# Down projection by seven products: evictions ahead of a step's operands, P2's weights resident, ring tiles asked for by ScalarE

## The chip, the core and the metric

The kernel runs on one core of one Trainium2 chip. The metric is the time of one execution in microseconds (us), the median of several runs. All times inside the kernel come from one profiled execution and count from the start of its span.

## The reference, cut to what matters

One inference step of a decoder layer for 1024 prompt positions and 8 samples (1032 columns in all). Its last part is a ConvFFN, and its last product is the one that the change concerns:

```python
def conv_ffn(x, g, w_up, conv_w, conv_b, w_down, buf):
    up = rmsnorm(x, g) @ w_up
    ext = jnp.concatenate([buf.astype(up.dtype), up], axis=1)
    conv = conv_b + sum(ext[:, i:i + t] * conv_w[i] for i in range(CONV_W))
    a, gate = jnp.split(conv, 2, axis=-1)
    y = (jax.nn.silu(gate) * a) @ w_down      # (1032 x 2816) @ (2816 x 1024)
    return y, ext[:, t:]
# and then  x = x + y
```

Everything is float32. The kernel works with the transpose: y has 1024 rows (output features) and 1032 columns (positions), the contraction runs over 2816 = 22 x 128 features.

## The kernel before, in words

**The stage.** The down projection is the last stage, from about 1097 us on. It is computed by Strassen's scheme: features, outputs and columns are each cut in two, and instead of eight half-size products there are seven, in the order P1, P2, P6, P7, P4, P5, P3 (`PHASE`, L483). Each product is a phase of 11 steps (`HK`), so there are 77 steps (`NSTEP`), numbered 0 to 76: P1 is 0 to 10, P2 11 to 21, P6 22 to 32, P7 33 to 43, P4 44 to 54, P5 55 to 65, P3 66 to 76. Here "P6 step 1" is the first step of P6, number 22.

**One step.** The operands are one weight tile (128 x 512) and one activation tile (128 x 516). For float32 accuracy each is split in a high and a low part. ScalarE makes the high parts `bh` (`b_hi`, L2034) and `wh` (`w_hi`, L2045) by copying with rounding; VectorE makes the low parts `bl` (`b_lo`, L2896) and `wl` (`w_lo`, L2901) by subtracting. There are four buffers of each (step number modulo 4), so `b_hi` of step n waits until TensorE is through with step n-4 (`p_done`). TensorE then does 24 matmuls of 128x128 by 258 columns (L1558 to L1560): four output blocks j, two column chunks, three products high-high, high-low, low-high. All eight banks of PSUM hold the four blocks j.

**Sums.** Most phases need sums or differences of tiles. VectorE makes them in place (`down_sum`, L2912): T1 to T4 of activation tiles, S1, S2, S2b, S3, S4 of weight tiles. Three lists say in which of its rounds VectorE makes each: `SUM_BEFORE` (ahead of `b_lo`), `SUM_BETWEEN` (between `b_lo` and `w_lo`), `SUM_BEHIND`. In round n VectorE makes bl and wl of step n. Of weight: S3 = w_a - w_b (in w_a), S2 = raw tile - w_a, S1 = w_b + raw tile, S4 = raw tile - w_a. S2 for step n+1 stands ahead of `b_lo(n)` in round n, S4 too.

**Weight tiles.** `w_a` (11 tiles) and `w_b` (11 tiles) are resident; `wr` is a ring of four raw tiles. In P2, P6, P4 and P3 the raw tile comes through the ring: SyncE asks for it (`ring_load`, L955) once step n-4 is done. So P2 uses the tile as it is, P4 too, P6 and P3 after S2 or S4.

**Between phases.** PSUM is emptied when a phase ends: after P1 by ScalarE (`p1_copy`, L2050, four copies to `u_p1`, written behind `w_hi` of step 13), after the others by VectorE (`evict`, L2984, four additions, block j each, written at the end of the round of the third step of the next phase, behind its `b_lo` and `w_lo`). TensorE waits for each bank before the first matmul of the next phase that writes it (`bank_free`, L1536). `pair_done` tells that a block j of a phase's last step is through.

**Order on the queues.** Each engine runs its instructions in the order written. SyncE (SP) issues, from 1108 us: the second halves of activation tiles (`act_load2`, L935, at most four in flight), tile 21, then `x_quarter` (L960, 1 MB each, the residual into xq0, xq1, xq2, each waiting until the one before has landed), and between them the ring tiles and `wb_load` (L948, w_b, one per P2 step). Later `y_store` (L965) writes finished quarters.

Of the kernel before, what the change touches and what calls it, by code (L numbers as in the profile page):

```python
# [98 lines left out]
def build(nc, t):  # L99
# [5 lines left out]
    with ctx:  # L105
# [391 lines left out]
        def weight(st):  # L497
            ph, k = PHASE[st // HK], st % HK
            return (w_a[k] if ph in ("P1", "P7") else w_b[k] if ph == "P5" else wr[st % 4])[:, :]

        RING_NO = {}
        for ph_ in ("P1", "P2", "P6", "P4", "P3"):
            for k_ in range(HK):
                RING_NO[step_of(ph_, k_)] = len(RING_NO)
# [3 lines left out]
        for k_ in range(HK):  # L508
            SUM_BEFORE[5 + k_ if k_ < 6 else 2 * k_ - 1].append(("T3", k_))
            SUM_BEHIND[5 + k_ if k_ < 6 else 2 * k_ - 1].append(("T2", k_))  # L510
            SUM_BEHIND[13 + k_].append(("S3", k_))
# [8 lines left out]
        VEC_NO = {}  # L520
        for st_ in range(NSTEP):
            for x_ in SUM_BEFORE[st_] + SUM_BETWEEN[st_] + SUM_BEHIND[st_]:
# [89 lines left out]
        def act_total(f):  # L612
            return 16 * (12 + f // 4 + 1)
        SET_END = {}
# [13 lines left out]
        def _(sp):  # L628
# [308 lines left out]
            def down_w(mi, f):  # L937
                return dnL[f, :, 512 * mi:512 * mi + 512]

# [5 lines left out]
            def wb_load(k):  # L945
                if k >= 4:
                    sp.wait_ge(S(f"tok_ld{k % 4}"), wb_total(k - 4))
                sp.dma_start(w_b[k][:, :], down_w(1, k)).then_inc(S(f"tok_ld{k % 4}"), 16)  # L948

            def ring_load(st):  # L950
                ph, k = PHASE[st // HK], st % HK
                mi = 1 if ph in ("P6", "P4") else 0
                n = RING_NO[st]
                sp.wait_ge(S("p_done"), NPROD + st - 3)
                sp.dma_start(wr[st % 4][:, :], down_w(mi, HK + k)).then_inc(S(f"ring_ld{n % 4}"), 16)  # L955
# [44 lines left out]
            for f in H2_ORDER[7:-1]:  # L1000
                act_load2(f)
# [4 lines left out]
            for st in range(HK, NSTEP):  # L1006
                ph, k = PHASE[st // HK], st % HK
                if st in RING_NO:
                    ring_load(st)
                if ph == "P2":  # L1010
                    if k == 1:
                        x_quarter(1, xq1, 0, 1)
                    if k == 3:
                        x_quarter(2, xq2, 1, 1)
                    wb_load(k)
# [551 lines left out]
        def _(act):  # L1567
# [454 lines left out]

            def b_hi(st):
# [12 lines left out]
            def w_hi(st):  # L2036
                ph, k = PHASE[st // HK], st % HK
                if ph in ("P1", "P2", "P4"):
# [1173 lines left out]
```

## Time and profile before

| | before |
|---|---|
| median of 3 runs | 1364.05 us (1361.47 to 1366.6) |
| the profiled execution's own time | 1361.91 us |
| its span | 1360.2 us |
| TensorE busy / VectorE / ScalarE | 95% / 78% / 44% of the span |
| DMA, mean over the span | 156 GB/s |

### The profile page before, as it was taken

How to read it: one execution, taken by the hardware profiler on the slowest of the kernel's cores; microseconds unless marked ns; L12 is line 12 of the kernel's file. 1: busy time of each engine (PE TensorE's matmuls, PEld its weight loads, DVE VectorE, ACT ScalarE, POOL GpSimd, SP SyncE). 2: the span in 40 equal slices, each digit the busy share in tenths (PEclk: the TensorE clock that was granted, in tenths of full speed). 3: DMA queues.
4: the chain of work that ended last, by engine and by line, in shares of the span. 5: the costliest groups of instructions: out<-in, count | busy, mean ns of one | idle time of the engine just before them, and what ended most of it. 6: DMA issues, size and time to landing. Idle time of an engine off the chain costs nothing.

```text
span 1360.2 us, 25417 instructions
## 1 busy us (share of the span) xinstructions
PE 1286.8 (95%) x9535; PEld 1181.0 (87%) x9535; DVE 1062.1 (78%) x1615; ACT 601.7 (44%) x1025; POOL 207.2 (15%) x207
## 2 busy tenths in 40 slices
PE   7999999989989999999999999999999996899988
PEld 5888787777667678899999999999999996899988
DVE  7678879988988767567687787788788885687955
ACT  7623111355657565344544434434434442333432
POOL 1420034322323430100101101101101000000000
PEclk9999999969999899999899999999999997999999
DMA  9878766689999773431221221221221497421212
GB/s 317 293 219 241 198 179 181 205 234 263 288 316 341 226 219 88 153 102 51 79 94 56 87 93 56 86 94 57 85 94 55 161 311 249 141 78 32 86 63 86
DMA packets 144279, 212.69 MB, mean 156 GB/s; under 512 B 13870, under 2 KB 93128, under 8 KB 143876
## 3 DMA queue, kind: packets, MB, share of 16 engines
q1 hardware_dynamic: 128564, 160.44, 37.8%
q0 software_dynamic: 10688, 38.80, 9.3%
q10 hardware_dynamic: 4904, 11.81, 3.1%
q8 instruction: 76, 1.25, 0.4%
q14 instruction: 47, 0.39, 0.1%
HBM read 180.68 MB, written 29.82 MB: 155 GB/s over the span
## 4 chain that ended last, share of the span: by engine, by line
PE 67%; DVE 13%; DMA 8%; issue 4%; SPq 3%; POOL 3%; ACT 1%; ACTq 1%; POOLq 0%; DVEq 0%
PE ps L1482 8%; PE ps L1483 8%; PE ps L1484 8%; PE ps L1558 5%; PE ps L1560 4%; PE ps L1559 4%; PE ps L1324 4%; PE ps L1265 3%; PE ps L1267 3%; PE ps L1266 3%; DMA upr<-in_w_upL 2%; PE ps L1347 2%; DMA wr<-in_w_down 1%; PE ps L1305 1%; DMA act<-scr_act 1%
## 5 line engine op out<-in xcount | busy, mean ns | idle before, releaser
L1558 PE MATMUL ps<-bh,wh 128*128 128x258 f32 x616 | 179.0, 291 | 30.1 <-DVE xq L2984 16.1
L1482 PE MATMUL ps<-hhi,uph 128*128 128x258 f32 x704 | 201.1, 286 | 1.6 <-DVE ug L2856 0.9
L1483 PE MATMUL ps<-hlo,uph 128*128 128x258 f32 x704 | 200.0, 284 | 0.0
L1484 PE MATMUL ps<-hhi,upl 128*128 128x258 f32 x704 | 199.7, 284 | 0.0
L1559 PE MATMUL ps<-bl,wh 128*128 128x258 f32 x616 | 176.5, 287 | 0.0
L1560 PE MATMUL ps<-bh,wl 128*128 128x258 f32 x616 | 175.9, 285 | 0.0
L1558 PEld LDWEIGHTS ps<-bh,wh 128*128 128x128 f32 x616 | 119.3, 194 | 31.4 <-issue 29.5
L1482 PEld LDWEIGHTS ps<-hhi,uph 128*128 128x128 f32 x704 | 134.3, 191 | 3.0 <-DVE ug L2856 2.0
L1483 PEld LDWEIGHTS ps<-hlo,uph 128*128 128x128 f32 x704 | 134.5, 191 | 0.0
L1484 PEld LDWEIGHTS ps<-hhi,upl 128*128 128x128 f32 x704 | 134.2, 191 | 0.0
L1265 PE MATMUL ps<-whi,hhi 128*128 128x512 f32 (+1 forms) x336 | 126.3, 376 | 0.9 <-PE ps L1267 0.6
L1267 PE MATMUL ps<-whi,hlo 128*128 128x512 f32 (+1 forms) x336 | 124.9, 372 | 0.0
L1266 PE MATMUL ps<-wlo,hhi 128*128 128x512 f32 (+1 forms) x336 | 124.6, 371 | 0.0
L1560 PEld LDWEIGHTS ps<-bh,wl 128*128 128x128 f32 x616 | 120.3, 195 | 0.0
L1559 PEld LDWEIGHTS ps<-bl,wh 128*128 128x128 f32 x616 | 120.1, 195 | 0.0
L1324 PEld LDWEIGHTS ps<-vst,pts 128*128 128x128 f32 x576 | 74.1, 202 | 31.5 <-issue 27.2
L3146 POOL TENSOR_TENSOR upr<-upr 128x512 f32<-128x512 f32 x22 | 29.5, 1343 | 450.5 <-DMA upr<-in_w_upL 367.5
L1900 ACT ACTIVATE uph<-upr 128x1024 fp32r<-128x1024 f32 (+1 forms) x66 | 79.3, 1202 | 41.7 <-DMA upr<-in_w_upL 37.4
L2776 DVE TENSOR_TENSOR upl<-upr,uph 128x1024 fp32r<-128x1024 f32 (+1 forms) x66 | 92.2, 1396 | 0.3 <-ACT uph L1900 0.2
L1324 PE MATMUL ps<-vst,pts 128*128 128x65 f32 x576 | 81.3, 289 | 9.2 <-DVE oN L2481 8.1
L2168 DVE TENSOR_TENSOR ring<-ring,qb 128x1024 f32<-128x1024 f32 x64 | 78.0, 1219 | 9.4 <-DMA ring<-in_cache_a_k 7.8
L3083 POOL DMA_INDIRECT vring<-in_cache_a_v,gtab x64 | 61.7, 964 | 140.4 <-PE ps L1347 136.4
(359 smaller groups left out, 3393.0 us busy)
## 6 DMA issues: line engine op xcount, KB each, us to landing
upr<-in_w_upL SPq DMA_DIRECT2D x88, 256.0 KB, 3.4
ring<-in_cache_a_k SPq DMA_DIRECT2D x170, 128.0 KB, 3.2
scr_act<-va SPq DMA_DIRECT2D x22, 516.0 KB, 2.6
wr<-in_w_down SPq DMA_DIRECT2D x44, 256.0 KB, 2.7
ring<-in_cache_a_k ACTq DMA_DIRECT2D x86, 128.0 KB, 3.0
act<-scr_act SPq DMA_DIRECT2D x36, 258.0 KB, 4.0
wst<-in_w_in SPq DMA_DIRECT2D x32, 256.0 KB, 3.9
x<-in_xT SPq DMA_DIRECT2D x16, 258.0 KB, 5.5
```

The source lines that it names most:

```text
L1265: pe.matmul(out, lh, whi[:, sl, 0:w], start=(kc == 0), stop=False)
L1266: pe.matmul(out, lh, wlo[:, sl, 0:w], start=False, stop=False)
L1267: i = pe.matmul(out, ll, whi[:, sl, 0:w], start=False, stop=(kc == KC - 1))
L1324: i = pe.matmul(ps[:, 6, 0:HD + 1], pts[:, g % 2, j, :], vst[:, hp % 2, j, VCOL[H % 2]], start=(j == 0), stop=(j == nb - 1))
L1482: pe.matmul(out, hi_, r_hi[:, cs], start=(first and i == 0), stop=False, skip_group_check=not first)
L1483: pe.matmul(out, hi_, r_lo[:, cs], start=False, stop=False, skip_group_check=not first)
L1484: m = pe.matmul(out, lo_, r_hi[:, cs], start=False, stop=(i == 3), skip_group_check=not first)
L1558: pe.matmul(out, hi_, bh[n][:, cs], start=(fresh and k == 0), stop=False, skip_group_check=not fresh)
L1559: pe.matmul(out, hi_, bl[n][:, cs], start=False, stop=False, skip_group_check=not fresh)
L1560: m = pe.matmul(out, lo_, bh[n][:, cs], start=False, stop=(k == HK - 1), skip_group_check=not fresh)
L1900: act.activation(uph[p % 2][:, a:b, :], upr[p % 2][:, a:b, :], ACT.Copy).then_inc(S("st_hi"), 1)
L2776: dve.tensor_tensor(upl[p % 2][:, a:b, :], upr[p % 2][:, a:b, :], uph[p % 2][:, a:b, :].bitcast(f32), ALU.subtract).then_inc(S("st_lo"), 1)
```

## The change

1. **Evictions.** The four evictions of a phase (all but P1's and P3's) move one round earlier and to the front: in the round of the second step of the next phase (two steps after the phase's last; `EVICT_AT`) VectorE evicts blocks 0 and 1, makes bl, evicts blocks 2 and 3, makes the sums in between, wl, and only then the sums that stood ahead of bl. ScalarE's four copies after P1 move likewise: two ahead of `b_hi(12)`, two between it and `w_hi(12)`.
2. **P2's weights resident.** The 11 raw tiles of P2 go into `w_b` ahead of the stage's second phase, each between two of the `act_load2` of SyncE; the ring no longer serves P2. The tiles that `w_b` held before (bottom weights for S3) are loaded over them, each once `w_lo` of the P2 step is made. S3 moves one round later (rounds 14 to 24, was 13 to 23), T3 and T2 one round later or two.
3. **Ring tiles asked for by ScalarE.** `ring_load` moves from SyncE's list to ScalarE's, directly ahead of `b_hi` of the same step, with the same condition (step n-4 done). The remaining 33 ring tiles (P6, P4, P3) go this way.

```diff
--- before.py
+++ after.py
@@ -496,19 +496,19 @@
 
         def weight(st):
             ph, k = PHASE[st // HK], st % HK
-            return (w_a[k] if ph in ("P1", "P7") else w_b[k] if ph == "P5" else wr[st % 4])[:, :]
+            return (w_a[k] if ph in ("P1", "P7") else w_b[k] if ph in ("P2", "P5") else wr[st % 4])[:, :]
 
         RING_NO = {}
-        for ph_ in ("P1", "P2", "P6", "P4", "P3"):
+        for ph_ in ("P1", "P6", "P4", "P3"):
             for k_ in range(HK):
                 RING_NO[step_of(ph_, k_)] = len(RING_NO)
         SUM_BEFORE = {st: [] for st in range(NSTEP)}
         SUM_BETWEEN = {st: [] for st in range(NSTEP)}
         SUM_BEHIND = {st: [] for st in range(NSTEP)}
         for k_ in range(HK):
-            SUM_BEFORE[5 + k_ if k_ < 6 else 2 * k_ - 1].append(("T3", k_))
-            SUM_BEHIND[5 + k_ if k_ < 6 else 2 * k_ - 1].append(("T2", k_))
-            SUM_BEHIND[13 + k_].append(("S3", k_))
+            SUM_BEFORE[6 + k_ if k_ < 5 else 2 * k_ + 1].append(("T3", k_))
+            SUM_BEHIND[6 + k_ if k_ < 5 else 2 * k_ + 1].append(("T2", k_))
+            SUM_BEHIND[14 + k_].append(("S3", k_))
             SUM_BEFORE[step_of("P6", k_) - 1].append(("S2", k_))
             SUM_BEFORE[step_of("P7", k_)].append(("T4", k_))
             SUM_BETWEEN[step_of("P4", k_)] += [("S1", k_), ("S2b", k_)]
@@ -518,8 +518,10 @@
         SUM_BEHIND[34].append(("x22", 0))
         SUM_BEHIND[38].append(("x21", 0))
         VEC_NO = {}
+        EVICT_AT = {step_of(ph_, HK - 1) + 2: ph_ for ph_ in PHASE[1:-1]}
         for st_ in range(NSTEP):
-            for x_ in SUM_BEFORE[st_] + SUM_BETWEEN[st_] + SUM_BEHIND[st_]:
+            first_, second_ = (SUM_BETWEEN, SUM_BEFORE) if st_ in EVICT_AT else (SUM_BEFORE, SUM_BETWEEN)
+            for x_ in first_[st_] + second_[st_] + SUM_BEHIND[st_]:
                 VEC_NO[x_] = 2 * FT + len(VEC_NO) + 1
         MV0, ST0 = 21, 3 * FT
         EVICT = ["P2", "P6", "P7", "P4", "P5", "P3"]
@@ -611,6 +613,8 @@
 
         def act_total(f):
             return 16 * (12 + f // 4 + 1)
+        def down_w(mi, f):
+            return t["w_down"][f, :, 512 * mi:512 * mi + 512]
         SET_END = {}
         for k_ in range(NV):
             if vset(k_)[2]:
@@ -934,25 +938,18 @@
                     sp.wait_ge(S("act_st"), 16 * FT)
                 sp.dma_start(act_t[f][:, col_half(1)], scr_act[f, :, col_half(1)]).then_inc(S(f"x_ld{i % 4}"), 16)
 
-            def down_w(mi, f):
-                return dnL[f, :, 512 * mi:512 * mi + 512]
-
             def wa_load(k):
                 if k >= 4:
                     sp.wait_ge(S(f"ring_ld{k % 4}"), ring_total(k - 4))
                 sp.dma_start(w_a[k][:, :], down_w(0, k)).then_inc(S(f"ring_ld{k % 4}"), 16)
 
-            def wb_load(k):
-                if k >= 4:
-                    sp.wait_ge(S(f"tok_ld{k % 4}"), wb_total(k - 4))
-                sp.dma_start(w_b[k][:, :], down_w(1, k)).then_inc(S(f"tok_ld{k % 4}"), 16)
-
-            def ring_load(st):
-                ph, k = PHASE[st // HK], st % HK
-                mi = 1 if ph in ("P6", "P4") else 0
-                n = RING_NO[st]
-                sp.wait_ge(S("p_done"), NPROD + st - 3)
-                sp.dma_start(wr[st % 4][:, :], down_w(mi, HK + k)).then_inc(S(f"ring_ld{n % 4}"), 16)
+            def wb_load(n):
+                if n >= 4:
+                    sp.wait_ge(S(f"tok_ld{n % 4}"), wb_total(n - 4))
+                if n >= HK:
+                    sp.wait_ge(S("st_lo"), ST0 + step_of("P2", n - HK) + 1)
+                src = down_w(0, HK + n) if n < HK else down_w(1, n - HK)
+                sp.dma_start(w_b[n % HK][:, :], src).then_inc(S(f"tok_ld{n % 4}"), 16)
 
             def x_quarter(i, dst, mi, ni):
                 if i:
@@ -997,22 +994,22 @@
             act_store(FT - 1)
             sp.wait_ge(S("aff"), 2 * FT)
             sp.dma_start(t["o_u10"], u10[:, :, :]).then_inc(S("out"), 16)
-            for f in H2_ORDER[7:-1]:
-                act_load2(f)
+            for k in range(HK):
+                wb_load(k)
+                if k < 10:
+                    act_load2(H2_ORDER[7 + k])
             sp.wait_ge(S("act_st"), 16 * FT)
             act_load(21)
             act_load2(21)
             x_quarter(0, xq0, 0, 0)
             for st in range(HK, NSTEP):
                 ph, k = PHASE[st // HK], st % HK
-                if st in RING_NO:
-                    ring_load(st)
-                if ph == "P2":
-                    if k == 1:
-                        x_quarter(1, xq1, 0, 1)
-                    if k == 3:
-                        x_quarter(2, xq2, 1, 1)
-                    wb_load(k)
+                if ph == "P2" and k == 1:
+                    x_quarter(1, xq1, 0, 1)
+                if ph == "P2" and k == 3:
+                    x_quarter(2, xq2, 1, 1)
+                if HK < st <= 2 * HK:
+                    wb_load(st - 1)
                 if st == step_of("P6", 3):
                     for j in range(4):
                         y_store("P2", j)
@@ -2020,6 +2017,12 @@
                 act.wait_ge(S("tap"), 6 * p + 4)
                 act.activation(vg[:, :], vg[:, :], ACT.Silu).then_inc(S("silu"), 1)
 
+            def ring_load(st):
+                ph, k = PHASE[st // HK], st % HK
+                n = RING_NO[st]
+                act.wait_ge(S("p_done"), NPROD + st - 3)
+                act.dma_start(wr[st % 4][:, :], down_w(1 if ph in ("P6", "P4") else 0, HK + k)).then_inc(S(f"ring_ld{n % 4}"), 16)
+
             def b_hi(st):
                 ph, k = PHASE[st // HK], st % HK
                 if st < 3:
@@ -2035,9 +2038,11 @@
 
             def w_hi(st):
                 ph, k = PHASE[st // HK], st % HK
-                if ph in ("P1", "P2", "P4"):
+                if ph in ("P1", "P4"):
                     n = RING_NO[st]
                     act.wait_ge(S(f"ring_ld{n % 4}"), ring_total(n))
+                elif ph == "P2":
+                    act.wait_ge(S(f"tok_ld{k % 4}"), wb_total(k))
                 elif ph in ("P6", "P3"):
                     act.wait_ge(S("s_vec"), VEC_NO["S2" if ph == "P6" else "S4", k])
                 elif ph == "P5":
@@ -2083,11 +2088,16 @@
             affine_a(FT - 1)
             silu(FT - 1)
             for st in range(4, NSTEP):
+                if st == HK + 1:
+                    p1_copy(0)
+                    p1_copy(1)
+                if st >= HK and st in RING_NO:
+                    ring_load(st)
                 b_hi(st)
+                if st == HK + 1:
+                    p1_copy(2)
+                    p1_copy(3)
                 w_hi(st)
-                if st == HK + 2:
-                    for j in range(4):
-                        p1_copy(j)
 
 
         @block.vector
@@ -2937,7 +2947,7 @@
                     dve.wait_ge(S("mv_lo"), MV0 + step_of("P6", k) + 1)
                     summed(top1, bot2, top1, ALU.subtract)
                 if name == "S3":
-                    dve.wait_ge(S(f"tok_ld{k % 4}"), wb_total(k))
+                    dve.wait_ge(S(f"tok_ld{(HK + k) % 4}"), wb_total(HK + k))
                     dve.wait_ge(S("st_lo"), ST0 + step_of("P1", k) + 1)
                     summed(wa, wa, wb, ALU.subtract)
                 if name == "S2":
@@ -3040,18 +3050,25 @@
             taps(FT - 1, ua, va, FT - 1, 2)
             gated(FT - 1)
             for st in range(4, NSTEP):
-                for name, k in SUM_BEFORE[st]:
-                    down_sum(name, k)
+                ph = EVICT_AT.get(st)
+                if ph:
+                    evict(ph, 0)
+                    evict(ph, 1)
+                else:
+                    for name, k in SUM_BEFORE[st]:
+                        down_sum(name, k)
                 b_lo(st)
+                if ph:
+                    evict(ph, 2)
+                    evict(ph, 3)
                 for name, k in SUM_BETWEEN[st]:
                     down_sum(name, k)
                 w_lo(st)
+                if ph:
+                    for name, k in SUM_BEFORE[st]:
+                        down_sum(name, k)
                 for name, k in SUM_BEHIND[st]:
                     down_sum(name, k)
-                ph = PHASE[(st - 3) // HK]
-                if (st - 3) % HK == HK - 1 and ph in EVICT:
-                    for j in range(4):
-                        evict(ph, j)
             for j in range(4):
                 evict("P3", j)
 
```

## Rows read from the trace of the kernel before

**Rows 1.** The page: the span, and TensorE's busy time, share and instructions

```profile
span 1360.2 us, 25417 instructions
PE 1286.8 (95%) x9535; PEld 1181.0 (87%) x9535; DVE 1062.1 (78%) x1615; ACT 601.7 (44%) x1025; POOL 207.2 (15%) x207
```

**Rows 2.** Timeline of TensorE, first matmuls of steps and the stage's last: start, length

```profile
1097.45 0.28 PE L1558 MATMUL ps<-bh,wh 128*128 128x258 f32 x1
...
1113.60 0.36 PE L1558 MATMUL ps<-bh,wh 128*128 128x258 f32 x1 [1.69 <-DVE wl L2901]
...
1143.12 0.55 PE L1558 MATMUL ps<-bh,wh 128*128 128x258 f32 x1 [12.14 <-ACT u_p L2050]
...
1147.94 0.28 PE L1558 MATMUL ps<-bh,wh 128*128 128x258 f32 x1
...
1150.81 0.28 PE L1558 MATMUL ps<-bh,wh 128*128 128x258 f32 x1
...
1182.07 0.55 PE L1558 MATMUL ps<-bh,wh 128*128 128x258 f32 x1 [5.39 <-DVE xq L2984]
...
1218.22 0.36 PE L1558 MATMUL ps<-bh,wh 128*128 128x258 f32 x1 [2.77 <-DVE xq L2984]
...
1254.00 0.36 PE L1558 MATMUL ps<-bh,wh 128*128 128x258 f32 x1 [2.59 <-DVE xq L2984]
...
1322.57 0.55 PE L1558 MATMUL ps<-bh,wh 128*128 128x258 f32 x1 [5.33 <-DVE xq L2984]
...
1356.49 0.28 PE L1560 MATMUL ps<-bh,wl 128*128 128x258 f32 x1
```

**Rows 3.** Stretches: us, busy of PE, PEld, DVE, ACT, POOL, PEclk, DMA share, GB/s

```profile
360.00:385.00 25.00, 21.21 (x190) 16.00 (x189) 21.66 (x45) 12.01 (x23) 8.98 (x9) 1.00 1.07 305
...
1114.00:1120.00 6.00, 6.00 (x53) 6.00 (x52) 6.00 (x11) 1.56 (x3) 0.00 (x0) 1.00 0.99 351
...
1126.00:1134.00 8.00, 4.98 (x42) 4.78 (x41) 1.38 (x3) 0.00 (x0) 0.00 (x0) 0.98 0.97 326
...
1322.57:1327.80 5.23, 5.23 (x24) 5.23 (x25) 1.66 (x3) 0.00 (x0) 0.00 (x0) 0.50 0.54 202
```

**Rows 4.** The chain that ended last, DMA pieces: start us, length us, what

```profile
1126.30 7.41 DMA xq<-scr_x
...
1134.70 7.14 DMA wr<-in_w_down
...
1176.71 2.61 DMA wr<-in_w_down
```

**Rows 5.** Timeline of VectorE, end of P2, and one sum over a quarter

```profile
1179.42 0.69 DVE L2912 TENSOR_TENSOR wr<-wr,wa 128x512 f32<-128x512 f32 x1 [0.24 <-DMA wr<-in_w_down]
...
1181.23 2.50 DVE L2984 TENSOR_TENSOR xq<-ps,xq 128x516 f32<-128x516 f32 x4
...
1213.35 2.31 DVE L2912 TENSOR_TENSOR xq<-xq,u_p 128x2064 f32<-128x2064 f32 x1
```

**Rows 6.** Timeline of VectorE and of ScalarE in P3: S4, then its w_hi

```profile
1330.78 0.69 DVE L2912 TENSOR_TENSOR wr<-wr,wa 128x512 f32<-128x512 f32 x1 [6.56 <-DMA wr<-in_w_down]
...
1331.51 0.63 ACT L2045 ACTIVATE wh<-wr 128x512 fp32r<-128x512 f32 x1 [2.77 <-DVE wr L2912]
```

**Rows 7.** Timeline of ScalarE where it issues DMAs (key pages, an earlier stage)

```profile
106.43 0.46 ACT L1657 ACTIVATE zo<-ps,rsx 128x256 f32<-128x256 f32 x1
106.58 1.35 ACTq L432 DMA_DIRECT2D ring<-in_cache_a_k  x2
...
250.86 0.47 ACT L1666 ACTIVATE sq<-ps,rsx 128x256 f32<-128x256 f32 x1
251.21 3.89 ACTq L432 DMA_DIRECT2D ring<-in_cache_a_k  x4
```

**Rows 8.** Issue to landing: the 44 ring tiles; the w_b tile issued at 1140.98

```profile
DMA to landing us min/median/max: 2.5/2.7/7.6
...
DMA to landing us min/median/max: 5.6/5.6/5.6
```

## The prediction, made before the changed kernel had run

> **What bounds the kernel now.** I read the page first: TensorE is busy for 95% of the span [rows 1], so only its idle time can be won. The timeline of TensorE then gives the places [rows 2]. A step takes 2.86 us when nothing waits: the next first matmul comes 1150.81 - 1147.94 = 2.87 later. The 77 steps go from 1097.45 to 1356.6 [rows 2]: 259.1 us, against 77 x 2.86 = 220.2, so some 39 us are lost. They lie at six places: step 5, 1.9; P1 to P2, 12.3; P2 to P6, 5.5; P6 to P7, 2.9; P7 to P4, 2.8; P5 to P3, 5.5 (the idle times in brackets plus 0.1 to 0.2 for the modelled tail of the last matmul), and 0.6 in two small ones. After four of them the clock has fallen: the first step of P3 takes 5.1 us at a granted 0.50, which is the 1.2 GHz level [rows 3]. That adds 2.0, 1.3, 1.6 and 2.6 us. The sum is 39.
>
> Why they wait: at the end of P2 (1176.7) SP asks for ring tile 25, which lands 2.6 later [rows 4], then come S2, bl, wl and only at 1181.23 the evictions [rows 5]. P2 itself starts late because its ring tiles stand behind 1 MB quarters on SP: 7.4 us for the first, then 7.1 for tile 13 behind the second [rows 4], and `p1_copy` stands behind `w_hi(13)`.
>
> **The change, part by part.** T is always the end of a phase's last step.
>
> *Step 5.* T3(0) leaves round 5, where it held bl(5) up until an activation half had landed. bl(5), wl(5) are then ready by 1110, and the step is due at 1111.7 instead of the 1113.6 of rows 2. Gain 1.9; no later T3 comes too late (round 6: wl at 1113.4, due 1114.6).
>
> *P1 to P2.* P2's weights are resident before step 11 (due 1128.9), and p1_copy stands ahead. Copies 0 and 1 follow blocks 0 and 1 of step 10, the last ends near 1130.0, `w_hi(12)` near 1130.5, wl(12) 1131.3, due 1131.8. So steps 11 to 14 run through, until 1140.3. But on SP the 11 new tiles (2.88 MB) stand ahead of the first quarter, and the DMA engines were moving 351 and 326 GB/s there, all but full [rows 3]: 8.2 to 8.8 us, less up to 1.7 for a slack stretch between. The first quarter landed at 1133.7 [rows 4]; now near 1141.0 (1140 to 1142). The second quarter waits for that, and `wb_load` for S3(0) stands behind it: issued 0.4 later and landing 5.6 later (the row of a w_b tile just behind a quarter [rows 8]), at 1147.0. S3(0) is in round 14, ahead of bl(15). VectorE then does S3, T3, bl, wl, each 0.61 apart: step 15 starts at 1149.7 instead of 1140.3, 9.4 us idle, and about 2.0 for the clock, as after the 12.1 before. The stall thus moves four steps back and shrinks from 14.3 to 11.4: gain 2.9 only. S3(2) waits once more, for a tile behind the third quarter, until about 1152.5; step 17 is due at 1157.4, so this is hidden. P2 ends at T = 1171.7, was 1176.5.
>
> *Evictions.* With blocks 0 and 1 evicted ahead of bl, behind what is in round n-1, the wait moves off TensorE's path. An eviction takes 0.62 (2.50 for four [rows 5]), a quarter of a step 0.72, so once the first is in time the others are. P6 to P7: VectorE is free, the first eviction ends 1.3 ahead of T, gain 4.5. P7 to P4: gain 2.8, less 0.25 for wl of P4 step 1, which now stands behind four evictions, bl, S1 and S2b (T+3.1, due T+2.9). P4 to P5: 0.1. P2 to P6 and P5 to P3: round n-1 holds S2 (S4) for a tile that ScalarE asked for only after `w_hi` of the step before; S2 ends at T-1.1, bl, wl at T+0.1, at P6 an S3 as well, then the eviction: TensorE starts at T+1.55 and T+0.9 instead of T+6.9 and T+8.1 (clock included): gain 5.35 and 7.2. In P7 the sum x22 (2.31 us [rows 5]) follows closely on the evictions and makes wl(35) 0.8 late.
>
> *Ring tiles by ScalarE: the term that decides.* SP asked for tile n as soon as step n-4 was done, whatever else went on. On ScalarE the request stands behind `w_hi(n-1)`. In P6 and P3 `w_hi(n-1)` waits for S2(n-1), that for its tile, and that for its request. So a circle closes, which the kernel before did not have:
> - S2 or S4 start to `w_hi` start: 0.73 (1330.78 to 1331.51 [rows 6]).
> - `w_hi` start to the DMA's issue: not in the trace for this pair. ScalarE issued key pages 0.15 and 0.35 after the start of the activation ahead of them, before it had ended [rows 7]. I take 0.25; no less than 0.15 is likely, and 0.65 if the issue waits for the 0.63 of the activation.
> - issue to the next S2: landing 2.7 in the median, 2.5 at least [rows 8]; tile 25 took 2.71 from TensorE's end (1176.71) to S2 (1179.42) [rows 4, 5]. Most of the spread lies above, so I take 2.87, and 3.0 as the upper end.
>
> Together 3.85 us a step (3.5 to 4.4) against TensorE's 2.86. Because S2(n+1) stands ahead of bl(n) and wl(n), TensorE has no reserve: step n starts 1.3 after S2(n+1) ends. P6: steps 22 and 23 on T+1.55 and T+4.5; S2(25) can only be asked for after S2(24), which now stands behind the evictions, so step 24 starts at T+10.2, 2.9 late; then seven steps at 3.85. A pause of 2.9 may cost the clock, as it did at P7 [rows 2]; the steps behind it have 1.0 of slack each, so I add nothing. P6 ends at T+43.3, plus 0.5 for the residual quarter beside it: 10.8 beyond its stall and its 31.4. P3 the same, from T+0.9: step 68 at T+9.6, end T+42.2, 9.9 beyond. In P4 `w_hi` needs the tile alone: circle 0.3+2.7+0.05 = 3.05, a lag of 0.2 a step, covered by the three steps of lead. The 33 issues themselves lie in ScalarE's idle time (44% busy [rows 1]). SP, rid of ring waits, gives out the residual quarter and the stores earlier; nobody waits for them.
>
> *Sum.* Gains: 1.9 + 2.9 + 5.35 + 4.5 + 2.8 + 0.1 + 7.2, and 0.5 for a small wait in P6: 25.3. Losses: 10.8 + 9.9 + 0.8 + 0.25 = 21.7. Net -3.6 us. Against the profiled execution's 1361.9 this is 1358.3; the three runs have their median at 1364.05, 2.1 higher, so I say 1360.4.
>
> No row speaks against ScalarE's queue as such. The Trainium skill ("DMA: Bandwidth & Descriptors", Issuing engines are not separate DMA queues) says that a request from another engine only saves the issuing sequencer's time. By that alone the move would be free and the sum would be 21 us lower. The page does not treat what stands ahead of the request.
>
> **The rivals.**
>
> *A. The requests don't hold each other up.* If ring tiles always land well ahead, P6 and P3 lose nothing: 1360.4 - 20.7 = 1339.7; with the quarters earlier too, 1328. For it: the same condition in the code. Against it: the order of ScalarE's list, which is not a question of size. 6 in 100.
>
> *B. Slower: the issue waits for the activation.* Then a circle is 0.73 + 0.65 + 3.0 = 4.4 and the 16 steps that hang on it cost 0.55 more each: +8.8. The pauses of 3.5 at step 24 and step 68 then bring the clock down as well, as a pause of 2.8 did at P7 and one of 2.6 did not [rows 2]; half is absorbed, since the steps behind have 1.5 of slack each: +2. That gives 1371. It decides from a circle of 4.3 on. Against it: rows 7. 11 in 100.
>
> *C. Slower still: the clock falls in every circle.* TensorE would pause about 1.0 of each 3.85 us. With 5.1 us for a step at 1.2 GHz [rows 3] the step would be longer than the circle: 16 x 1.3 = 21 more, 1381. Against it: from 360 to 385 TensorE was 85% busy in short pieces and the clock stayed 1.00 [rows 3]; at 74% it is less sure. 4 in 100. The Trainium skill ("TensorE: Matmul & The Clock Gate", HAM oscillation — how this bites in real kernels) describes a loop whose wait for a DMA throttles the engine anew in each round. That was with longer waits than compute; here the wait is the shorter.
>
> *D. A shorter circle, 3.5 to 3.6, or quarters that land at 1139.* A circle of 3.55 takes 16 x 0.3 = 4.8 off, quarters 2 us earlier some 1.5 more: 1354. It is the lower end of my own terms. 19 in 100.
>
> **How the numbers follow.** The forecast with its terms near their values has 60 in 100: 1360.4, from 1354 to 1367. With half of D's and B's reach the range is 1352 to 1369. A measurement of this kernel can tell about 0.5% (6.8 us) from no change. Faster by more than that, below 1357.2 us (0.995 times 1364.05): A, D and a tail of the forecast, 0.28. Slower, above 1370.9: B's upper part, C, 0.12. Within: 0.60.
>
> **What would show it.** P2: idle time of TensorE not at step 11 but at step 15, about 9 us, released by wl behind an S3 that waited for w_b's tile. P6 and P3: first matmuls of steps 25 to 31 and 69 to 75 some 3.85 apart, VectorE's S2 and S4 waiting for the ring tile each time, and ScalarE's request right behind `w_hi`. P7, P4, P5: steps 2.86 apart, no pause at their starts but 0.8 at P7's third step. PEclk 1.00 in P6 and P3. The prediction is wrong if ring requests go out ahead of `w_hi` of the step before, if the circle is under 3.6 or over 4.1, or if the first quarter lands before 1139.

## The result, and the profile after

The changed kernel takes 1352.0 us (median of 7, 1348.2 to 1356.0) against 1364.05 (median of 7, 1361.5 to 1370.4): ratio 0.991, 95% interval 0.988 to 0.993. That is 12 us less, where the forecast was 3.6 less and "within 0.5%" the likeliest; 1352.0 lies on the lower end of the stated range. The mechanism that the forecast rested on is in the trace; its price was too high.

The span is 1349.3 us, against 1360.2 [rows 1]. This is the whole stage as one stretch, first of the kernel before and then of the changed one (columns: stretch, length, busy time of TensorE, weight loads, VectorE, ScalarE, GpSimd, then granted clock, DMA share, GB/s):

```profile
1097.45:1356.61 259.16, 229.04 (x1850) 227.67 (x1848) 182.54 (x281) 90.12 (x157) 0.00 (x0) 0.95 0.38 123
```

```profile
1094.92:1345.50 250.58, 230.82 (x1850) 226.81 (x1848) 181.18 (x281) 90.13 (x157) 0.00 (x0) 0.97 0.38 128
```

The stage is 8.6 us shorter, with the same work in it. It also starts 2.5 us earlier, though everything ahead of it is the same program: that part is no effect of the change (more on it below, with the second traces). The timeline of TensorE, first matmuls of steps 15, 22, 24, 27, 33, 35, 44, 66, 68 and 74; it answers [rows 2]:

```profile
1147.09 0.55 PE L1555 MATMUL ps<-bh,wh 128*128 128x258 f32 x1 [8.64 <-DVE wl L2911]
...
1170.75 0.36 PE L1555 MATMUL ps<-bh,wh 128*128 128x258 f32 x1 [1.13 <-DVE xq L2994]
...
1178.97 0.36 PE L1555 MATMUL ps<-bh,wh 128*128 128x258 f32 x1 [1.94 <-DVE wl L2911]
...
1191.04 0.36 PE L1555 MATMUL ps<-bh,wh 128*128 128x258 f32 x1 [0.93 <-DVE wl L2911]
...
1210.51 0.28 PE L1555 MATMUL ps<-bh,wh 128*128 128x258 f32 x1
...
1217.17 0.36 PE L1555 MATMUL ps<-bh,wh 128*128 128x258 f32 x1 [0.78 <-DVE wl L2911]
...
1242.96 0.28 PE L1555 MATMUL ps<-bh,wh 128*128 128x258 f32 x1
...
1306.70 0.36 PE L1555 MATMUL ps<-bh,wh 128*128 128x258 f32 x1 [0.27 <-DVE xq L2994]
...
1314.94 0.36 PE L1555 MATMUL ps<-bh,wh 128*128 128x258 f32 x1 [1.96 <-DVE wl L2911]
...
1336.18 0.36 PE L1555 MATMUL ps<-bh,wh 128*128 128x258 f32 x1 [0.50 <-DVE wl L2911]
```

Read against [rows 2]: the 12.1 at step 11 has become 8.6 at step 15; the 5.4, 2.8, 2.6 and 5.3 at the starts of P6, P7, P4 and P3 have become 1.1, nothing, nothing and 0.3. New are a pause of 1.9 at the third step of P6 and of P3 and one of 0.2 to 0.9 at most of the steps after it, all released by `wl`. So P6 and P3 stretch to 39.8 and 38.8 us, where 11 x 2.86 is 31.4. The stretches of P6 and P3 show TensorE busy for 89% and 90%, the clock near full:

```profile
1170.75:1210.51 39.76, 35.32 (x264) 33.68 (x265) 26.95 (x42) 13.12 (x23) 0.00 (x0) 0.96 0.31 107
1306.70:1345.50 38.80, 34.78 (x264) 33.46 (x264) 21.76 (x35) 9.88 (x17) 0.00 (x0) 0.96 0.27 88
```

The pause at step 15 has its reason on SyncE and in the chain. The first quarter lands 8.59 after its request; only then does `wb_load` get its turn, and S3(0) on VectorE has waited 11.82 us for that tile (chain of the changed kernel, then timeline of VectorE):

```profile
1129.92 8.59 DMA xq<-scr_x
...
1138.98 5.42 DMA wb<-in_w_down
...
1144.43 0.69 DVE L2922 TENSOR_TENSOR wa<-wa,wb 128x512 f32<-128x512 f32 x1 [11.82 <-DMA wb<-in_w_down]
```

And this is the circle, in P3: S4 on VectorE, `w_hi` and the next request on ScalarE, and the next S4 when the tile has landed (timelines of VectorE and ScalarE, in order of time):

```profile
1330.54 0.69 DVE L2922 TENSOR_TENSOR wr<-wr,wa 128x512 f32<-128x512 f32 x1 [1.70 <-DMA wr<-in_w_down]
...
1331.26 0.63 ACT L2050 ACTIVATE wh<-wr 128x512 fp32r<-128x512 f32 x1 [2.44 <-DVE wr L2922]
1331.27 0.33 ACTq L2024 DMA_DIRECT2D wr<-in_w_down  x1
...
1334.13 0.69 DVE L2922 TENSOR_TENSOR wr<-wr,wa 128x512 f32<-128x512 f32 x1 [1.69 <-DMA wr<-in_w_down]
...
1334.86 0.63 ACT L2050 ACTIVATE wh<-wr 128x512 fp32r<-128x512 f32 x1 [2.44 <-DVE wr L2922]
1334.86 0.34 ACTq L2024 DMA_DIRECT2D wr<-in_w_down  x1
```

It goes round in 3.59 us here, and between 3.3 and 3.6 elsewhere, with two exceptions in P6. One turn of 4.0 holds the sum x12. One of 4.8, from 1176.92 to 1181.68, holds a tile that took 3.93 to land: the last 1 MB quarter had gone out on SyncE 2.46 us ahead of it (timeline of SyncE, then chain):

```profile
1175.20 0.38 SPq L957 DMA_DIRECT2D xq<-scr_x  x1
...
1177.66 3.93 DMA wr<-in_w_down
```

The link that no row of before showed, from `w_hi` to the request, is 0.00 to 0.01 us in every turn.

### The profile page after: what moved, and what is told of

Its sections match the earlier page's. It is cut to its first block, busy times and chain, and to the rows that moved or that the text cites. A ratio compares the mean times of both kernels' runs of the same rounds, so it can differ in the third digit from the quotient of the medians.

```text
span 1349.3 us, 25428 instructions
## 1 busy us (share of the span) xinstructions
PE 1287.0 (95%) x9535; PEld 1178.0 (87%) x9535; DVE 1058.6 (78%) x1615; ACT 601.5 (45%) x1025; POOL 207.9 (15%) x207
## 4 chain that ended last, share of the span: by engine, by line
PE 54%; DVE 17%; DMA 13%; issue 5%; SPq 5%; POOL 4%; ACT 2%; ACTq 1%; DVEq 0%; another core or an unknown queue 0%; POOLq 0%
PE ps L1479 9%; PE ps L1480 8%; PE ps L1481 8%; DMA wr<-in_w_down 4%; PE ps L1321 3%; PE ps L1555 3%; PE ps L1557 2%; PE ps L1556 2%; POOL rsn L3087 2%; DMA upr<-in_w_upL 2%; PE ps L1344 2%; DMA ring<-in_cache_a_k 2%; DMA act<-scr_act 1%; PE ps L1420 1%; PE ps L1302 1%
## 5 line engine op out<-in xcount | busy, mean ns | idle before, releaser
L1321 PEld LDWEIGHTS ps<-vst,pts 128*128 128x128 f32 x576 | 72.0, 197 | 32.2 <-issue 28.2
```

The costliest lines, as they stand in the source:

```text
L1321: i = pe.matmul(ps[:, 6, 0:HD + 1], pts[:, g % 2, j, :], vst[:, hp % 2, j, VCOL[H % 2]], start=(j == 0), stop=(j == nb - 1))
```

## The experiments

Theory: the request on ScalarE closes a circle with `w_hi` and S2 or S4, and the place of the quarters on SyncE makes the pause at step 15. Below, "stage" is the time from the first matmul of step 0 to the end of step 76 in each kernel's own trace, and a phase lasts from its first matmul to that of the next. The table stands ahead of the single runs; ratios are to the kernel before on the same chip, with their 95% intervals.

| kernel | median us | ratio | stage | P1 | P2 | P6 | P7 | P4 | P5 | P3 |
|---|---|---|---|---|---|---|---|---|---|---|
| before | 1364.05 | 1 | 259.2 | 45.7 | 39.0 | 36.2 | 35.8 | 31.6 | 37.0 | 34.0 |
| changed | 1352.0 | 0.991 (0.988 to 0.993) | 250.6 | 31.9 | 43.9 | 39.8 | 32.5 | 31.9 | 31.9 | 38.8 |
| e1, SyncE asks | 1336.7 | 0.980 (0.975 to 0.985) | 239.2 | 31.7 | 46.0 | 33.5 | 32.5 | 31.9 | 31.4 | 32.2 |
| e2, before + ScalarE asks | 1374.6 | 1.009 (1.006 to 1.012) | 272.3 | 44.7 | 45.0 | 42.5 | 34.3 | 31.6 | 38.8 | 35.4 |
| e3, before + evictions | 1332.8 | 0.976 (0.972 to 0.980) | 233.9 | 39.6 | 34.0 | 32.5 | 32.5 | 31.9 | 31.4 | 32.1 |
| e4, before + resident | 1360.0 | 0.998 (0.995 to 1.000) | 258.9 | 31.6 | 51.1 | 38.3 | 35.7 | 31.6 | 36.8 | 33.8 |
| e5, behind b_hi | 1351.1 | 0.992 (0.990 to 0.995) | 249.9 | 32.2 | 43.1 | 40.6 | 32.5 | 31.9 | 31.7 | 38.0 |
| e6, quarters later | 1341.1 | 0.983 (0.980 to 0.987) | 241.5 | 31.8 | 35.5 | 40.0 | 32.5 | 31.9 | 31.7 | 38.1 |
| e8, ahead of w_hi | 1343.6 | 0.986 (0.982 to 0.990) | 237.8 | 31.6 | 43.3 | 35.4 | 32.5 | 31.9 | 31.4 | 31.8 |
| e9, e6 and e8 | 1330.9 | 0.979 (0.976 to 0.983) | 229.6 | 32.1 | 34.8 | 34.9 | 32.4 | 31.9 | 31.4 | 32.1 |
| e10, after w_hi's end | 1361.8 | 1.000 (0.998 to 1.003) | 262.7 | 31.5 | 45.2 | 44.3 | 32.5 | 33.1 | 32.5 | 43.8 |
| e11, all causes out | 1327.9 | 0.975 (0.971 to 0.979) | 224.8 | 31.4 | 33.7 | 33.0 | 31.4 | 31.9 | 31.4 | 32.0 |

**e1_ring_sp: only the requests go back to SyncE.**

```diff
 # ScalarE
-                if st >= HK and st in RING_NO:
-                    ring_load(st)
 # SyncE, for st in range(HK, NSTEP)
+                if st in RING_NO:
+                    ring_load(st)      # sp.wait_ge(p_done ...); sp.dma_start(wr ...)
```

> The changed kernel with one part undone: the 33 ring tiles are asked for by SyncE again, with the same condition; evictions and resident weights stay as changed. Theory (circle): w_hi, request, landing and S2 or S4 hold each other on ScalarE's list, and P6 and P3 take 39.8 and 38.8 us in the changed kernel's trace against 11 x 2.86 = 31.4. Without the circle both take 31.4 to 32.5, the pauses at their starts shrink from 1.3 and 0.4 to 0.5 or less: some 15 us less than the changed kernel, 1337 us, ratio to the kernel before 0.980. Rival (landing): the steps of P6 and P3 are late because the tile itself lands late, whoever asks, and VectorE's order does the rest; then P6 and P3 stay at 38 to 40 and the time at 1352. Both: step 15 still starts about 9 us late.

1336.7 us: 15 less than the changed kernel. The stage tells what of this is the circle's: it is 11.4 shorter, with 6.3 less in P6, 6.6 less in P3 and 2.1 more in P2. The other 4 us lie ahead of the stage or in the scatter, where nothing was edited, so that the time came out as expected is luck in part. The phases decide: P6 and P3 fell by over 6 us each, as the circle says and the rival does not. Here they are without it (stretches):

```profile
1169.61:1203.11 33.50, 33.36 (x265) 33.16 (x265) 26.77 (x42) 13.26 (x23) 0.00 (x0) 0.95 0.34 119
1298.87:1331.09 32.22, 31.93 (x266) 31.52 (x264) 21.44 (x35) 9.79 (x17) 0.00 (x0) 1.00 0.32 104
```

TensorE is busy for 99%. One thing was not as expected: the pause at P6's start did not shrink from 1.3 to 0.5 but grew to 3.5, with a slow step behind it, so P6 missed its 31.4 to 32.5 by 1.0. The timeline of SyncE says why:

```profile
1157.75 0.33 SPq L958 DMA_DIRECT2D wr<-in_w_down  x1
1163.06 0.33 SPq L952 DMA_DIRECT2D wb<-in_w_down  x1
1163.44 3.21 SPq L958 DMA_DIRECT2D wr<-in_w_down  x3
```

The second ring tile of P6 stands behind the last w_b load, which waits for `wl` of step 21 (made at 1162.30, timeline of VectorE). SyncE's list has a hold-up of its own at this place, and this one the move to ScalarE does take away.

**e2_ring_act: the kernel before, only the requests on ScalarE.**

```diff
 # SyncE
-                if st in RING_NO:
-                    ring_load(st)
 # ScalarE, for st in range(4, NSTEP)
+                if st >= HK and st in RING_NO:
+                    ring_load(st)
                 b_hi(st)
```

> The kernel before with the ring requests moved to ScalarE, nothing else. Theory (circle): a circle of about 3.45 us a step exists here too, but each phase begins with a pause in which operands of two or three steps get ready. Evictions stand behind a tile asked for after w_hi(24), so the pauses at P6 and P3 grow by some 1.8 each; after them a lead of about 6 us covers 10 x 0.6 us of lag, so P6 and P3 lose little more. P2's tiles no longer stand behind the quarters on SyncE: step 11 starts up to 4 us earlier, then P2's steps may lag by 0.3 each. In all 1362 to 1369, ratio 0.998 to 1.004. Rival (no reserve anywhere): P6 and P3 lose their 8 us each here as well, 1378 to 1382, ratio 1.012.

1374.6, ratio 1.009: between the two, and neither. P3's own steps lose only 1.4 us, but P6 loses 6.3 and P2 6.0, and the pauses ahead of P6 and P3, which the table counts in P2 and P5, grow from 5.5 to 6.5 and from 5.5 to 7.3. So the lead after a long pause does cover much of the circle in P3, and I had set it too high for P6 and P2. P6 differs from P3 by one landing. Its fifth ring tile was asked for 0.52 us after a 1 MB quarter on SyncE and took 5.21 to land; the same tile of P3, with no quarter beside it, took 2.60 (timeline of SyncE, then chain):

```profile
1186.04 0.38 SPq L953 DMA_DIRECT2D xq<-scr_x  x1
...
1186.56 5.21 DMA wr<-in_w_down
...
1333.55 2.60 DMA wr<-in_w_down
```

Those 2.6 us used up the lead (TensorE pauses 1.7 at step 25), and the steps behind it lag as in the changed kernel. Alone, the part costs 12 us, 13.1 of the stage, and it is the only one of the three that costs anything alone.

**e3_evict: the kernel before, only the evictions and P1's copies moved.**

```diff
+                ph = EVICT_AT.get(st)
+                if ph:
+                    evict(ph, 0)
+                    evict(ph, 1)
 ...                                   # b_lo, evict 2 and 3, w_lo, sums, and ScalarE's p1_copy, as in the change
-                ph = PHASE[(st - 3) // HK]
-                if (st - 3) % HK == HK - 1 and ph in EVICT:
-                    for j in range(4):
-                        evict(ph, j)
```

> The kernel before with the eviction part alone: evictions and P1's copies where the change puts them, ring by SyncE, P2 through the ring. Theory: the pauses at P6, P7, P4 and P3 (6.9, 4.6, 2.8 and 8.1 with the clock) fall to under 0.7 each, x22 costs 0.8 to 1.1, and step 11 starts some 7 us earlier since P1's copies no longer stand behind w_hi(13), which waits for a ring tile; part of that comes back as a pause at step 13 or later. In all 19 to 27 us less than before, 1337 to 1345, ratio 0.981 to 0.986: better than the whole change. Rival (the parts need each other): without the resident weights and the requests by ScalarE the evictions bring no more than the whole change did, 12 us, ratio 0.991.

1332.8, 4 us below the expected range: 30 us less than before, 19 less than the whole change. The stage is 25.3 shorter than before, which the expected 19 to 27 held, and 16.7 shorter than the changed kernel's. The pauses of TensorE at P2's and P6's start:

```profile
1134.31 0.55 PE L1560 MATMUL ps<-bh,wh 128*128 128x258 f32 x1 [5.25 <-DVE wl L2906]
...
1168.26 0.36 PE L1560 MATMUL ps<-bh,wh 128*128 128x258 f32 x1 [0.49 <-DVE xq L2989]
```

P1 to P2 waits 5.3 instead of 12.1 with the old ring tiles; of this edit only P1's copies, ahead of `w_hi(12)`, bear on it. Evictions and P1's copies bring all of the gain, and the two other parts together give 16.7 us of the stage back. Three kernels split this: e3, e1 (resident weights added) and the changed kernel (requests by ScalarE added) have stages of 233.9, 239.2 and 250.6, so the resident weights cost 5.3 on top of the evictions and the requests 11.4.

**e4_resident: the kernel before, only P2's weights resident** (and T3, T2, S3 later). Against e1 it has the evictions where they were:

```diff
 # against e1_ring_sp
-        EVICT_AT = {step_of(ph_, HK - 1) + 2: ph_ for ph_ in PHASE[1:-1]}
 ...                                   # VectorE's rounds and P1's copies as in the kernel before
```

> The kernel before with the resident weights of P2 alone (and the later T3, T2, S3 that belong to them). Theory (the stall moves): step 5's 1.9 goes, steps 11 to 14 run through except a pause under 1 at step 11, and step 15 waits about 9 us for S3(0), whose tile stands behind the first two quarters on SyncE, plus 2 for the clock. The four other pauses stay. Net 3 to 5 us less than before, 1359 to 1361, ratio 0.997. Rival (the stall is removed): P1 to P2 costs nothing more, 14 to 16 us less, 1349, ratio 0.989.

1360.0, ratio 0.998, as the moved stall says, though the stage is only 0.3 shorter than before: step 15 waits 9.1 us. But the pause at P6 grew too, from 5.5 to 8.5: SyncE's hold-up of e1 again. The phases' sums tell it shortly: P1 is 14.1 shorter, P2 12.1 longer, P6 2.1 longer.

**e5_behind_bhi: the request one activation later.**

```diff
-                if st >= HK and st in RING_NO:
-                    ring_load(st)
                 b_hi(st)
+                if st >= HK and st in RING_NO:
+                    ring_load(st)
```

> The changed kernel with ScalarE's request written behind b_hi of its step instead of ahead of it, a dose: the circle grows by one activation, 0.53 us (the distance from w_hi to b_hi in the changed kernel's trace), from about 3.45 to 3.98 a step. Theory (circle): the 16 steps that hang on it cost 0.53 more each, 8.5 us; P6 goes from 39.8 to 44 us, P3 from 38.8 to 43, the time to 1360, ratio to the kernel before 0.998. Rival (the steps are late for another reason, the landing alone): nothing changes, P6 and P3 within 1 us, 1352.

Nothing changed (1351.1). By its letter the rival is right; but the timeline of ScalarE shows that the dose was not given:

```profile
1182.03 0.63 ACT L2050 ACTIVATE wh<-wr 128x512 fp32r<-128x512 f32 x1 [2.74 <-DVE wr L2922]
1182.12 0.34 ACTq L2024 DMA_DIRECT2D wr<-in_w_down  x1
1182.57 0.62 ACT L2037 ACTIVATE bh<-act 128x516 fp32r<-128x516 f32 x1
```

The request went out 0.09 us after `w_hi` began, while `b_hi`, which stands ahead of it on the list, began only at 1182.57. It was 0.09 to 0.10 for every request of P6 but the first, and 0.00 to 0.01 in P3. A `b_hi` whose waits are met holds the request behind it up by at most 0.1 us, not by its length. So the dose had to be a wait that is not met.

**e10_after_whi: the request waits until w_hi has ended.**

```diff
                 act.wait_ge(S("p_done"), NPROD + st - 3)
+                act.wait_ge(S("st_hi"), ST0 + st)
                 act.dma_start(wr[st % 4][:, :], ...)
```

> The changed kernel with one wait more: ScalarE's request for tile n waits until w_hi(n-1) has ended, instead of going out while it runs. A dose that the last one turned out not to be (its request went out 0.09 us after w_hi began, though an activation stood between). Theory (circle): 0.65 us more in each circle, 3.5 becomes 4.15, 16 steps hang on it: P6 and P3 5 us longer each (45 and 43), P4 at most 1, stage 261 us against 250.6, time 1362, ratio 0.999. Rival (the landing alone paces P6 and P3): stage under 254.

1361.8: the whole gain of the change is gone. The timeline of ScalarE in P3 and the stretches of P6 and P3:

```profile
1336.88 0.63 ACT L2051 ACTIVATE wh<-wr 128x512 fp32r<-128x512 f32 x1 [2.24 <-DVE wr L2923]
1337.59 0.34 ACTq L2025 DMA_DIRECT2D wr<-in_w_down  x1
...
1340.98 0.63 ACT L2051 ACTIVATE wh<-wr 128x512 fp32r<-128x512 f32 x1 [2.37 <-DVE wr L2923]
```

```profile
1170.22:1214.51 44.29, 35.19 (x265) 33.59 (x265) 27.05 (x42) 14.01 (x23) 0.00 (x0) 0.96 0.29 97
1312.57:1356.33 43.76, 35.03 (x264) 33.53 (x264) 21.78 (x35) 10.76 (x17) 0.00 (x0) 0.96 0.25 82
```

The request now goes out 0.71 after `w_hi` began, the circle is 4.1, and P6 and P3 grow by 4.5 and 5.0 us. Dose and effect fit: 16 steps x 0.7 is 11, the stage grew by 12.1 (P6 and P3 9.5, P2 1.3, P4 and P5 1.8). The rival is out.

**e8_ahead: the request for tile n+1 ahead of w_hi(n), still on ScalarE.**

```diff
-                if st >= HK and st in RING_NO:
-                    ring_load(st)
                 b_hi(st)
 ...
+                if st + 1 >= HK and st + 1 in RING_NO:
+                    ring_load(st + 1)
                 w_hi(st)
```

> The changed kernel with ScalarE's request for step n+1 ahead of w_hi(n) instead of behind it; ScalarE still asks. Theory (it is the order on the list, not the engine): the circle is cut, P6 and P3 take 32 to 33 us instead of 39.8 and 38.8, and the pause at P6's start stays under 1 since the request doesn't stand behind the w_b loads of SyncE as it did with SyncE asking (3.5). 14 to 15 less than the changed kernel: 1337 to 1338, stage 236 us, ratio 0.981. Rival (ScalarE's issue itself costs, or w_hi(n), now held until step n-3 is done, comes too late): P6 and P3 above 36.

P3 takes 31.75 us in all, clock 1.00:

```profile
1175.92:1211.33 35.41, 33.56 (x264) 33.18 (x265) 26.70 (x42) 13.29 (x23) 0.00 (x0) 0.95 0.36 119
1307.09:1338.84 31.75, 31.75 (x266) 31.51 (x264) 21.60 (x35) 9.80 (x17) 0.00 (x0) 1.00 0.33 105
```

So it is the place on the list, not the engine. The stage fell by 12.8 of the expected 14 to 15; P6 took 35.4, over the expected 32 to 33 and just under the rival's 36. It keeps a pause of 2.0 at step 26, where a ring tile asked for at 1182.24 is used by VectorE only at 1187.67, 5.4 later instead of 2.7: the fourth quarter (1 MB) went out at 1180.38. The pause at P6's start was 1.3, not under 1. The time, 1343.6, is 6 above what was expected; the stage explains 2 of these.

**e6_quarters, e9_ahead_quarters: the quarters behind the w_b loads; and both repairs together.**

```diff
-            x_quarter(0, xq0, 0, 0)           # ahead of the loop
 ...                                          # and numbers 1 and 2 at P2's steps 1 and 3
                 if HK < st <= 2 * HK:
                     wb_load(st - 1)
+                if st in (16, 19, 22):
+                    i = (16, 19, 22).index(st)
+                    x_quarter(i, (xq0, xq1, xq2)[i], (0, 0, 1)[i], (0, 1, 1)[i])
```

> The changed kernel with the three residual quarters later on SyncE's list: behind the w_b loads of steps 15, 18 and 21 instead of ahead of those of steps 11 and 13. Theory (queue order on SyncE makes the pause at step 15): the tile for S3(0) lands by 1135 instead of 1144, the pause of 8.8 at step 15 and its 2.2 for the clock are gone, P2 takes 32 to 34 us instead of 43.9, P6 and P3 stay at 39 to 40 each. 10 to 11 less: 1341, ratio 0.984. Rival (bandwidth makes it): the loads are as many as before, so the pause only moves within P2, and P2 stays above 40.

> Both: the request ahead of w_hi and the quarters later. If the two causes are apart their gains add: stage 225 to 227 us (77 steps of 2.86 are 220.2), 25 less than the changed kernel, 1327, ratio 0.973. If either takes the other's gain over, 1333 or more.

e6: 1341.1, and P2 35.5 instead of 43.9 with the clock at 1.00 (stretch of P2):

```profile
1130.46:1165.96 35.50, 32.07 (x266) 31.54 (x265) 27.03 (x45) 14.42 (x26) 0.00 (x0) 1.00 0.74 253
```

P2 is a little over the expected 32 to 34, by pauses of 1.1 at step 15 and 1.5 at step 21. P1 and P2 together moved 18.9 MB in 67.3 us, the changed kernel's 19.6 MB in 75.8 (GB/s of the stretches times their length; here the third quarter was asked for only at 1162.04 and lands mostly behind P2). So nearly the same bytes crossed in 8.5 us less, and the pause did not move within P2: it was the order on SyncE. VectorE still waits for the tile of S3(0), but 4.2 us and not 11.8, and TensorE 1.1 and not 8.8. e9: 1330.9, stage 229.6 against 225 to 227 expected: the gains of e6 (9.1) and e8 (12.8) give 21.9 if they add, and 21.0 were measured. The two causes are apart.

**e11_best: all of it.** As in e1, but each ring tile asked for two steps further up on SyncE's list (ahead of the next w_b load), two quarters behind w_b loads, the other two in P7 with their sums in rounds 40 and 43.

```diff
                 if HK < st <= 2 * HK:
                     wb_load(st - 1)
+                if st + 2 in RING_NO:
+                    ring_load(st + 2)          # by SyncE
+                if st in (16, 19):
+                    x_quarter((16, 19).index(st), ...)
+                if st == step_of("P7", 0):
+                    x_quarter(2, xq2, 1, 1)
 ...                                    # quarter 3 and the sum x21 likewise later
-        SUM_BEHIND[34].append(("x22", 0))
+        SUM_BEHIND[40].append(("x22", 0))
```

> What the runs point to, in one kernel: evictions and resident weights as changed; ring tiles asked for by SyncE, each ahead of the w_b load that would hold it up; the first two residual quarters behind the w_b loads of steps 15 and 18, the third and fourth in P7, their sums in rounds 40 and 43 where VectorE is free. Theory: P1 31.8, P2 33 to 35, P6 31.8 to 32.5, P7 31.5, P4 31.9, P5 31.4, P3 31.9; stage 224 to 226 us of at least 220.2, 24 to 26 below the changed kernel: 1325, ratio 0.973. Rival (the causes hide behind each other): 229 or more, as with the request ahead of w_hi.

The stage as one stretch:

```profile
1100.72:1325.52 224.80, 221.68 (x1850) 220.53 (x1848) 180.90 (x281) 89.53 (x157) 0.00 (x0) 1.00 0.42 142
```

224.8 us with the clock at 1.00 throughout, of 220.2 that 77 steps take at the least; P6 is 33.0, a little over the expected 31.8 to 32.5. The time is 1327.9, ratio 0.975. It beats both kernels. That it is faster than e9 or e3 rests on the stage (4.8 and 9.1 us shorter) more than on the times, whose intervals overlap.

**The second traces.**

> The kernel before once more, for a second trace: does the stage repeat, and does what lies ahead of it? The starts of the stage lay between 1090.5 and 1101.1 us in ten kernels that are the same up to there. Expected: stage 259.2 within 2 us, its start anywhere in that range. If the stage itself moved by 4 us or more, differences between phases of that size would mean nothing.

> The changed kernel once more, likewise: stage 250.6 within 2 us, P6 39.8 and P3 38.8 within 1, the pause at step 15 within 1 of 8.8.

The stage took 258.3 us before and 249.4 after, 0.9 and 1.2 from the first traces; P6 and P3 of the changed kernel 39.6 and 38.0. So the stage's gain repeats: 8.6 in the first pair, 8.9 in the second, 7.7 and 9.8 if the pairs are crossed. These two executions took 1358.7 and 1349.8 us, 8.9 apart, all of it in the stage. Where the stage starts does not stand firm: 1090.5 to 1101.1 us in fourteen traces of twelve kernels that are the same up to there. Median time less stage lies between 1097.5 (e1) and 1105.8 (e8), in no order with what was edited. The measured 12 us are therefore some 8.7 from the stage and some 3 that no part of the change was shown to cause; a difference of 2 or 3 us between medians says little by itself.

## Why the prediction was right or wrong

**The circle, mechanism right, price wrong.** The order was as told: `w_hi`, request, landing, S2 or S4. The term that failed is "`w_hi` start to the DMA's issue", put at 0.25 with 0.15 as the least likely bound: it is 0.00 to 0.01. The pairs of [rows 7] that I took it from read a page number (line 432 of the kernel) in front of the request; that this took the 0.15 and 0.35 is likely, but no run shows it. The other mis-sized term is "issue to the next S2", 2.87 for 2.55 to 2.86. Together 3.85 for some 3.5 us. Over 16 steps that is 5 to 6: P6 took 39.8 from its first matmul where the forecast had 42.25, P3 38.8 where it had 41.3. These 5.0 us are all that the stage gained over the forecast (8.6 for 3.6). That it comes out so evenly is luck in part: by its own terms the forecast's P6 ends at T+42.9 and not at T+43.3 (10.2 + 7 x 3.85 + 2 x 2.86), and the quarter beside it cost one turn 1.3 where I had 0.5. The rival D, a circle of 3.5 to 3.6, is what came.

**P1 to P2, right.** The pause moved to step 15 and was 8.8 (forecast 9.4), with 2.3 for the clock (forecast 2.0). The first quarter landed at 1138.5 and S3(0) began at 1144.4; counted from the start of the stage, 43.6 and 49.5, where the forecast had 43.6 and 49.6.

**Evictions, right.** Starts of P6 and P3 at 1.3 and 0.4 late (1.55 and 0.9), none at P7 and P4, 0.36 at P4's second step (0.25), 0.95 at step 35 for x22 (0.8). e3 shows the part alone, worth all of the gain.

**Step 5, right, less 0.4.** Its 1.9 went; 0.4 came back at step 6, where T3(0) now stands.

**Step 24 and 68.** 2.1 late, not 2.9, by the shorter circle. The clock fell there after all (15 matmuls of 0.42 us instead of 0.28 each time), and as said the slack of the steps behind took most of it.

**Rivals.** B (the issue waits for the activation) was given the price 1371; e10 built it and measured 1361.8, since the rest of the circle was cheaper as well. C (the clock falls in each circle) did not come: 0.96 over P6 and P3, with the fall at step 24 and 68 alone. A is not what happened, but e8 shows that it was one line away. The rule named there, that the issuing engine makes no difference to the transfer (the Trainium skill, "DMA: Bandwidth & Descriptors", Issuing engines are not separate DMA queues), agrees with e8 against e1 in P3, 31.75 for 32.2 us; what it does not speak of, the place on the list, cost 12.8 us of the stage (changed kernel less e8).

**The signs that I had named.** Ring requests did go out behind `w_hi`, as forecast. But the circle was under 3.6, which I had named as a sign of being wrong, and the first matmuls of steps 25 to 31 and 69 to 75 were 2.9 to 4.0 apart, not 3.85. PEclk was 0.96 in P6 and P3, not 1.00. The first quarter landed at 1138.5, before 1139, but only because this trace's stage started 2.5 earlier.

**The verdict.** "Within 0.5%" was wrong: 0.9% faster. Of the 8.4 us between forecast and result 5.0 are the circle's price; 3.4 lie ahead of the stage or in the scatter. I had taken the shift between one profiled execution and the median for constant, and given neither this scatter nor a circle at 3.5 enough of the chance.

## What to carry to other kernels

A load request that is moved to another engine's list inherits every unmet wait ahead of it there. If one of those waits hangs, through another engine, on the load asked for before, the loads that ran four deep run one deep, at landing time plus the links: draw the circle, sum its links, and compare it with the step. Put the request for the next tile ahead of the instruction that waits for this one. And undo a bundled change part by part, from both ends: here one part shortened the stage by 25.3 us and the other two gave 16.7 of them back. What a part costs depends on what stands beside it: the resident weights cost nothing alone and 5.3 us beside the evictions, since they then trade a pause of 5.3 us at P2's start for one of 8.2 at step 15.

## What the runs showed of the hardware

ScalarE does not hold a DMA request back until the activations ahead of it have ended, where the request's own wait is met. In the circle it went out 0.00 to 0.01 us after the start of the activation directly ahead. With a second activation between it was 0.09 to 0.10 in P6 and 0.00 to 0.01 in P3 (e5), before that second one had begun. When it had to wait for the first one's end it was 0.71 to 0.73 (a length of 0.63).

A 256 KB tile of the circle landed and was in use 2.55 to 2.9 us after its request. With a 1 MB load gone out ahead by the other engine it was more: 5.2 to the landing alone when that was 0.5 us ahead (e2), 5.4 to its use when 1.9 (e8), 3.9 to the landing when 2.5 (changed kernel).

After a pause of TensorE of 1.9 us ahead of the same step 24 the granted clock fell to the 1.2 GHz level in one execution and not in the other (15 matmuls of 0.42 us, and none; 0.28 is the length at the 2.4 GHz level):

```profile
1178.97:1183.43 4.46, 4.46 (x24) 4.41 (x24) 2.20 (x4) 1.02 (x2) 0.00 (x0) 0.62 0.41 147
```

```profile
1178.00:1182.00 4.00, 2.93 (x24) 2.93 (x24) 2.02 (x4) 0.91 (x2) 0.00 (x0) 1.00 0.71 270
```

The first is the changed kernel's first trace, the second its second. In the fourteen traces of this stage every pause above 5 us (by the bracket) was followed by 12 to 27 slow matmuls. Of the 24 pauses of 1.8 to 3.5 us 12 were followed by 13 to 16 and 12 by none, and after those of 1.7 or less there was never more than one.
